# Gating products behind the result sums, a second home for their convolution, and a reordered head in the block slots of a gated MLP

## The reference

```python
x = x + conv_gated_mlp(rmsnorm(x, g_ffn), w_up, conv_w, conv_b, w_down)

def conv_gated_mlp(h, w_up, conv_w, conv_b, w_down):
    up = h @ w_up                                     # 1024 -> 2 * 2816
    pad = jnp.pad(up, ((0, 0), (1, 1), (0, 0)))
    conv = sum(pad[:, j:j + s] * conv_w[j] for j in range(3)) + conv_b
    a, b = jnp.split(conv, 2, axis=-1)
    return (jax.nn.gelu(a) * b) @ w_down
```

## Time and profile before

| | |
|---|---|
| median of 3 runs | 1733.42 us (1733.41 to 1733.48) |
| profiled execution | 1733.78 us, span 1732.0 us |
| PE busy | 1680.2 us, 97% of the span, 8873 matmuls |
| DVE busy | 1067.2 us, 62% |
| ACT busy | 833.7 us, 48% |
| POOL busy | 775.6 us, 45% |
| granted TensorE clock | full in all 40 slices |
| HBM read and written | 170.92 MB, 10.50 MB |

### The profile page before, as it was taken

One profiled execution on the slowest core, in us unless ns is written; L12 is line 12 of the kernel. 1 busy time (PEld: TensorE's weight loads), 2 busy tenths in 40 slices (PEclk: granted clock), 3 DMA queues, 4 the chain that ended last, 5 costly groups with the idle time before them and its releaser, 6 DMA issues.

```text
span 1732.0 us, 23983 instructions
## 1 busy us (share of the span) xinstructions
PE 1680.2 (97%) x8873; PEld 1444.5 (83%) x8873; DVE 1067.2 (62%) x1664; ACT 833.7 (48%) x1509; POOL 775.6 (45%) x784
## 2 busy tenths in 40 slices
PE   9999999999999899999999999999999998999998
PEld 7888888888887799988888888888888877998886
DVE  4778875533347888861146888755333587888922
ACT  4766753222344466652255766432223445666422
POOL 3443343423353677744344343343334447766422
PEclk9999999999999999999999999999999999999999
DMA  7323222224232232242352222322242332323432
GB/s 259 119 74 98 74 98 97 74 97 145 97 122 97 75 106 90 97 158 91 95 190 98 74 74 88 108 74 97 97 145 97 121 98 74 98 98 98 144 106 79
DMA packets 147317, 182.75 MB, mean 106 GB/s; under 512 B 3040, under 2 KB 130706, under 8 KB 146194
## 3 DMA queue, kind: packets, MB, share of 16 engines
q1 hardware_dynamic: 147090, 181.35, 31.5%
q10 hardware_dynamic: 128, 0.09, 0.0%
HBM read 170.92 MB, written 10.50 MB: 105 GB/s over the span
## 4 chain that ended last, share of the span: by engine, by line
PE 78%; DVE 15%; ACT 4%; issue 3%; DMA 0%; ACTq 0%; DVEq 0%; SPq 0%
PE banks L1812 15%; PE banks L1814 15%; PE banks L1813 15%; PE banks L2049 3%; PE banks L1847 3%; PE banks L1848 3%; PE banks L1849 3%; PE banks L2054 3%; PE banks L2050 3%; DVE g_f L1525 2%; DVE conv L1520 2%; DVE conv L1517 2%; PE banks L2127 2%; PE banks L2128 2%; PE banks L2129 2%
## 5 line engine op out<-in xcount | busy, mean ns | idle before, releaser
L621 POOL TENSOR_TENSOR w_lo<-raw,w_hi 128x256 fp32r<-128x256 f32 x636 | 507.5, 832 | 813.6 <-ACT w_hi L711 813.6
L1812 PE MATMUL banks<-xg_hi,w_hi 128*128 128x512 f32 x896 | 351.2, 392 | 13.3 <-issue 9.8
L1813 PE MATMUL banks<-xg_lo,w_hi 128*128 128x512 f32 x896 | 349.2, 390 | 0.0
L1814 PE MATMUL banks<-xg_hi,w_lo 128*128 128x512 f32 x896 | 348.9, 389 | 0.0
L1253 DVE TENSOR_TENSOR w_lo<-raw,w_hi 128x768 fp32r<-128x768 f32 (+2 forms) x118 | 105.7, 896 | 176.3 <-ACT w_hi L710 175.9
L1812 PEld LDWEIGHTS banks<-xg_hi,w_hi 128*128 128x128 f32 x896 | 168.3, 188 | 51.0 <-issue 12.4
L1814 PEld LDWEIGHTS banks<-xg_hi,w_lo 128*128 128x128 f32 x896 | 168.2, 188 | 35.6
L1813 PEld LDWEIGHTS banks<-xg_lo,w_hi 128*128 128x128 f32 x896 | 168.4, 188 | 33.3 <-issue 0.2
L710 ACT ACTIVATE w_hi<-raw 128x768 fp32r<-128x768 f32 (+2 forms) x119 | 87.3, 733 | 176.4 <-PE banks L1814 86.2
L711 ACT ACTIVATE w_hi<-raw 128x1280 fp32r<-128x1280 f32 (+3 forms) x119 | 158.8, 1334 | 0.0
L664 POOL TENSOR_TENSOR a_lo<-raw,a_hi 128x1024 fp32r<-128x1024 f32 (+1 forms) x56 | 109.8, 1961 | 84.9 <-ACT a_hi L1016 84.9
(11 more groups left out here) (234 smaller groups left out, 3827.7 us busy)
## 6 DMA issues: line engine op xcount, KB each, us to landing
raw<-in_w_in SPq DMA_DIRECT2D x55, 1024.0 KB, 5.1
raw<-in_w_up SPq DMA_DIRECT2D x44, 1024.0 KB, 5.1
raw<-in_w_br SPq DMA_DIRECT2D x16, 1024.0 KB, 5.0
raw<-in_w_down SPq DMA_DIRECT2D x12, 1024.0 KB, 5.0
x_spill<-x_res SPq DMA_DIRECT2D x4, 2048.0 KB, 7.4
x_res<-x_spill SPq DMA_DIRECT2D x4, 2048.0 KB, 9.3
raw<-in_w_out SPq DMA_DIRECT2D x8, 1024.0 KB, 5.0
raw<-in_w_down SPq DMA_DIRECT2D x8, 896.0 KB, 4.7
```

Of the source, the lines that this page charges most:

```text
L621: last = nc.gpsimd.tensor_tensor(w_lo[p_][:, k, :], raw[p_][:, k, :], f32(w_hi[p_][:, k, :]), ALU.subtract)
L1812: nc.tensor.matmul(out, w_hi[w][:, k, cols], x_hi[:, a, :], start=first and k == 0, stop=False)
L1813: nc.tensor.matmul(out, w_hi[w][:, k, cols], x_lo[:, a, :], start=False, stop=False)
L1814: mm = nc.tensor.matmul(out, w_lo[w][:, k, cols], x_hi[:, a, :], start=False, stop=last and k == kt - 1)
```

## The change

`x_res` is free from the spill to the reload. The convolution of b in the blocks is now computed in its second and fourth request half (`conv_of`), so that the gating product of both halves can be issued behind the two sums. In the head, ACT rounds slot 2 between the halves of slot 0, later slots as before at an iteration's end, and stages block 0 an iteration earlier; DVE subtracts the weights' low part behind the first evacuation of a slot, and does normalise, h_sum and operand_lo ahead of the convolution instead of behind it. The core of the diff:

```diff
+    def conv_of(z, half):
+        return conv[half][:, :, :] if z % 2 == 0 or z < 0 else x_res[:, 2 * half:2 * half + 2, SEQ:2 * SEQ]
...
             def reload():
                 sp.wait_ge(block_done, 7 * (l + 1) * SZ)
+                sp.wait_ge(gated_ok, (l + 1) * FSLOT * 2)
                 sp.dma_start(x_res[:, :, :], x_spill2.ap()).then_inc(reloaded2, 16)
...
             def gelu(i, half):
+                if l + i:
+                    sc.wait_ge(gated_ok, (l * FSLOT + i - 1) * 2 + (half + 1))
...
             def stage(z):
                 if z == 0:
                     sc.wait_ge(h_ok, l * KT + KT)
+                    sc.wait_ge(spilled2, 16 * l + 16)
...
             def block_hi(z, n):
+                if n == 2 and z == 0:
+                    sc.wait_ge(h_lo_pool, l * 3 + 3)
...
             def block_centre(z, half):
-                if ab == 0:
+                if ab or z == 0:
                     sc.wait_ge(gated_ok, (l * FSLOT + i - 1) * 2 + half + 1)
-                if ab:
-                    sc.wait_ge(act_ok, (l * FSLOT + i) * 2 + half + 1)
-                nc.scalar.activation(conv[half][:, :, :], half_out(z, half), ACT.Identity,
+                else:
+                    sc.wait_ge(act_ok, (l * FSLOT + i - 1) * 2 + half + 1)
+                if z == 1:
+                    sc.wait_ge(spilled2, 16 * l + 16)
+                nc.scalar.activation(conv_of(z, half), half_out(z, half), ACT.Identity,
...
             for n in range(NS):
-                if n < NS - 1:
-                    split(S_F + n + 1)
                 if n == 0:
+                    split(S_F + 1)
                     round_sum(2 * l + 1)
...
                 for half in range(2):
                     conv_centre(n, half)
                     if n % 2 == 0:
                         gelu(n // 2, half)
+                    if half == 0:
+                        if n == 0:
+                            split(S_F + 2)
+                        if n == NS - 2:
+                            stage(0)
+                        if n == NS - 1:
+                            for b in range(4):
+                                block_hi(0, b)
+                    elif n < NS - 2:
+                        if n:
+                            split(S_F + n + 2)
...
-                if ab:
-                    ve.wait_ge(conv2_ok, k)
-                    ve.wait_ge(act_ok, (l * FSLOT + i) * 2 + (half + 1))
-                    nc.vector.tensor_tensor(g_f32[:, t, :], act[half][:, :, :].rearrange("p r n -> p (r n)"),
-                                            c[:, :, :].rearrange("p r n -> p (r n)"), ALU.mult).then_inc(gated_ok, 1)
+            def multiply(z, half):
+                n = NS + z
+                k, i = conv_count(1, n // 2, half), n // 2
+                ve.wait_ge(conv2_ok, k)
+                ve.wait_ge(act_ok, (l * FSLOT + i) * 2 + (half + 1))
+                nc.vector.tensor_tensor(g_f32[:, 2 * i + half, :].rearrange("p (r n) -> p r n", r=REQS), act[half][:, :, :],
+                                        conv_of(z, half), ALU.mult).then_inc(gated_ok, 1)
...
             for z in range(1, SZ):
                 if z < SZ - 1:
                     block_adds(z + 1)
                 for half in range(2):
-                    convolve((z - 1) % 2, i, half, half_out(z - 1, half))
+                    convolve(z - 1, half, half_out(z - 1, half))
                     if z < SZ - 1 and half == 0:
                         block_low(z + 1)
                 if z == SZ - 1:
                     split(S_D)
-                    gated_lo(0)
                 block_sums(z)
-            for t in range(1, 4):
+                if z % 2 == 0:
+                    for half in range(2):
+                        multiply(z - 1, half)
+            for t in range(4):
                 gated_lo(t)
             for half in range(2):
-                convolve(1, FSLOT - 1, half, half_out(SZ - 1, half))
+                convolve(SZ - 1, half, half_out(SZ - 1, half))
                 gated_lo(4 + half)
+            for half in range(2):
+                multiply(SZ - 1, half)
             split(S_D + 1)
```

More of the change, by code:

```diff
@@ L1062, in _ @@
                         gelu(n // 2, half)
[L1063 to L1074 removed]
+                    for q in H_ACT[{(3, 0): slice(0, 3), (3, 1): slice(3, 5), (4, 0): slice(5, 7)}.get((n, half), slice(0, 0))]:
+                        operand_hi(q)
+                    if half == 0:
[9 more added lines that the diff above has]
+                            split(S_F + n + 2)
             stage(1)
@@ L1554, in block_adds @@
                     ve.wait_ge(h_lo_vector, l * 4 + 4)
-                    ve.wait_ge(h_lo_pool, l * 3 + 3)
+                    ve.wait_ge(h_t_ok, l * 4 + 4)
                 elif z < 3:
@@ L1584, in gated_lo @@
                                         f32(g_hi[:, 2 * t:2 * t + 2, :]), ALU.subtract).then_inc(g_lo_ok, 2)
+            split(S_F + 1)
+            low_sum(2 * l + 1)
+            ve.wait_ge(rms_ok, 2 * l + 2)
             for n in range(NS):
-                if n < NS - 1:
-                    split(S_F + n + 1)
-                if n == 0:
-                    low_sum(2 * l + 1)
-                    ve.wait_ge(rms_ok, 2 * l + 2)
                 for half in range(2):
                     evacuate(n, half)
-                    if n == NS - 1 and half == 0:
-                        block_adds(0)
-                    if n == NS - 1 and half == 1:
-                        block_adds(1)
-                    convolve(n % 2, n // 2, half, up_bank(n, half).rearrange("p (r n) -> p r n", r=REQS))
-                    if n == 1:
-                        for m in range(2 * half, 2 * half + 2):
-                            normalise(m)
-                    if n == 2:
-                        for m in range(4 + 2 * half, 6 + 2 * half):
+                    if 1 <= n <= 2:
+                        for m in range(4 * n + 2 * half - 4, 4 * n + 2 * half - 2):
                             normalise(m)
@@ L1609, in _ @@
                         operand_lo(H_VECTOR[2 * (n - 4) + half])
+                    if half == 0 and n < NS - 1 and n:
+                        split(S_F + n + 1)
+                    if n == NS - 2 and half == 1:
+                        block_adds(0)
                     if n == NS - 1 and half == 0:
                         block_low(0)
+                    if n == NS - 1 and half == 1:
+                        block_adds(1)
+                    convolve(n - NS, half, up_bank(n, half).rearrange("p (r n) -> p r n", r=REQS))
+                    if n % 2:
+                        multiply(n - NS, half)
             block_low(1)
```

20 lines of the change are left out of this document (3 added, 17 removed).

## The result

The changed kernel takes **1747.39 us** (1743.47 to 1747.81, 4 runs) against 1733.45 us (1733.41 to 1734.32, 4 runs) for the kernel before on the same chip: ratio 1.0074, 95% interval 1.0057 to 1.0092. It is 14 us slower. The forecast was 1730.4 us in a range of 1718 to 1740, so the time lies outside of it. The profiled execution took 1747.56 us (span 1745.8).

The account below looks back on a forecast made before the run. TensorE (PE), busy 97% of the span, was taken as the bound, so only shorter PE waits help. Terms -23.1 + 21.7 - 11.6 + 0 + 10.0 = -3.0 us from 1733.42 gave 1730.4 us, range 1718 to 1740.

Parts of the forecast that it names:

- even blocks: Blocks 2, 4, ..., 12: gating products move behind both sums, so twelve PE waits before the seventh product go; -23.1 us.
- odd blocks: Five odd blocks per layer: the late third seed makes PE wait before the fifth product; 10 x 2.17 = +21.7 us.
- head: Slots 2 to 7 of each layer: waits for weight parts shrink from 8.0 to 2.2 us per layer; -11.6 us.
- block 0: First block of each layer: 14.3 us against 14.4, so nothing; bounds -3 to +3 us for both layers.
- tail: After block 13: later reload of x_res delays the next weights; 4.4 us in layer 0, 5.6 in the last; +10.0 us.
- PE waits 2.13 us, plus 0.04 for the restart: Odd blocks, before the fifth product: PE's wait for the third seed plus restart, 2.17 us each time.
- the chain itself: Odd blocks: held fourth addition ends at 6.0 us, then ACT's rounding (1.38) and third seed (0.39), ending at 7.84.
- The hold: A DVE operation with both inputs in SBUF, issued while POOL runs, ends 0.55 us after that POOL instruction.
- rival (a): Odd blocks not held: first product beats POOL's last subtraction, started 0.15 us earlier; 21.7 us not lost, 1708.7 us; chance 0.13.
- Rival (c): Head: DVE's low part of the weights late at every slot, six slots losing 1.5 us each; 1744.6 us; chance 0.15.
- (b): Tail hidden: weights come with the first free engines, or the products run earlier; 1721 us; chance 0.10.

## Why the prediction was wrong

| term | forecast | from the profiles |
|---|---|---|
| even blocks | -23.1 | 12 x (10.13 - 12.05) = -23.0 |
| odd blocks | +21.7 | 10 x (13.74 - 10.13) = +36.1 |
| head | -11.6 | -6.4 (layer 0), -6.5 (layer 1) = -12.9 |
| block 0 | 0 | 15.65 + 15.66 - 14.43 - 14.37 = +2.5 |
| tail | +10.0 | 4.5 + 6.5 = +11.0 |
| sum | -3.0 | +13.7 (spans: +13.8) |

(The head of layer 1 is block 13 to block 0, 707.82 us against 709.77, less the 4.5 us of the tail within it.)

- **The step that failed** is the one that reads "PE waits 2.13 us, plus 0.04 for the restart", and with it "10 x 2.17 = +21.7 us". The wait was right, 2.07 us. The restart was mis-sized: it costs 1.5 us, because the granted clock falls behind a wait of this length. Shown by the extra matmuls, which leave the wait and give 14 to 15 us back, and by the longer waits of the kernel before. I had priced the restart from waits of 1.71 us, where it is 0.2 at most, and carried it to one that was 0.2 us longer than any of those. No rival spoke of the clock. With 1.5 us per odd block the sum would have been +11.6. (In the chain itself 6.05 + 1.38 + 0.39 is 7.82, not 7.84; and 2.13 is 0.05 more than 7.84 - 5.76: that is the step from the seed's end to the product, which the changed kernel has too, 7.78 and 7.83.)
- **Even blocks**, right to 0.1 us: shown by the twelve waits gone and blocks of 10.13 us.
- **The hold**, right. The fourth addition ended 5.99 us into the block, and two placements that let it start before POOL made it 0.69 us. On rival (a), which spoke of 0.15 us on POOL: the first product was held, and the additions started 0.03 us from the forecast.
- **Block 0**, forecast at nothing, cost 2.5 us. It is the same loss. PE's idle time is not more than before, but it comes in two pieces of 0.76 and 2.85 us instead of three, of which the longest was 1.99 and left the clock up. The clock of 592 to 598 us is 0.72 in the changed kernel. Two traces have the same wait with the clock up, both in layer 1: the run with 14 extra matmuls and the one with one product behind. Their block 0 lasts 14.17 us, which is near the 14.3 of the forecast; the clock costs the other 1.5 us of each 15.65.
- **Without the clock** the change would have been slightly faster. An estimate from these blocks: +13.8 - 10 x (13.74 - 12.25) - 2 x (15.66 - 14.17) = -4.1 us, against the forecast of -3.0. So one missing term made nearly all of the error.
- **Head** and **tail** were off by 1.3 and 1.0 us. The walk of the head was too careful at slots 3 to 5, where PE doesn't wait at all. Rival (c), a low part late at every slot, did not come, nor did (b): the weights landed 10.3 us after their issue, where 10.8 was taken from the row. The term of layer 1, 5.6 us, is not added up from its parts (1.2 and 3.1) in the prediction; it measured 6.5.
- The clock also fell once in each tail: the granted clock is 0.59 from 772.8 to 777 us and 0.62 from 1640 to 1644.5, behind waits of 1.93 and 2.7 us. In layer 0 that adds nothing to be seen: with the products behind the additions the clock stayed up behind a wait of 1.92 us there, and block 13 to block 0 took 707.71 us, against 707.82. In layer 1 no run separates it, so that a part of the 6.5 us may be the clock's.
- By the 436 GB/s of the Trainium skill (DMA: Bandwidth & Descriptors, section Where 436 GB/s comes from) the tail would have cost about 3 us; it cost 11. The same section says that for transfers from HBM a limit of about 358 GB/s binds, which the prediction left out; as an estimate from it, 3.0 MB need 8.4 us. The trace is near the lower rate: from 762 to 770.9 us, up to the landing of the weights, the DMA queues moved 370 GB/s.
- The range was too narrow by 7 us. It held bounds for block 0, head and tail, but none for the largest positive term, whose chain was read from rows while its last link, the engine's pace behind the wait, was taken as fixed.

What stays open: why a wait of this length costs the clock in most blocks and not in all. Waits of 1.93 us in two odd blocks of layer 1 left it up in one run, 1.99 us did in block 0 of the kernel before, 2.85 us in two blocks 0, and 1.8 us cost it in 11 of 12 even blocks of another. In the head, on the other hand, all nine waits of 1.76 to 1.81 us in the kernel before and its variants left it up. The length of the wait alone does not decide it. No run separated what else does.

## What to carry to other kernels

A stall that moves from one place to another is not priced by its length alone. One unharmed stall of the same length proves little: the trace of before had one of 1.99 us with the clock up, and the new ones of 1.92 us all lost it. What could be relied on was the length that passed every time in the same kind of place (twelve of 1.71 us in front of a product). Beyond such a length, put one clock loss per stall into the range, 1.5 us here, and look at the granted clock and the pace of the matmuls behind the stall. Before an operation is moved on one engine, list which of its neighbours have both inputs in SBUF and where POOL's instructions start; the same work put a few instructions later (behind the additions instead of in front of them) was worth 35 us here. And in a queue that works in order, put what another engine needs soonest (the seed) ahead of what waits longest (the rounding): that alone gave 29 us.

## What the runs showed of the hardware

- The granted clock can fall behind a short stall. Twelve waits of 1.71 us in the kernel before left it at 1.00 and cost 0.2 us beyond themselves, and ten of 1.4 us left it up too. Waits of 1.8 to 2.0 us cost the clock in 32 of 36 even blocks, those of 1.92 and 1.93 us in 18 of 20 odd ones, and those of 2.85 us in 12 of 14 blocks 0. The loss was 1.5 us at 1.8, 1.9 and 2.0 us and did not grow with the wait. In block 0 it varied: 1.2 to 1.5 us in ten, and 2.6 to 2.7 in two, whose clock stayed down for longer (16.81 and 16.89 us instead of 14.17). The Trainium skill (TensorE: Matmul & The Clock Gate, section What's actually happening) says that the chip gates this clock to half by how busy the engine has been; the trace agrees: matmul starts 0.21 us apart instead of 0.12, and a granted clock of 0.57 to 0.66 in stretches of both levels.
- Idle time can be filled to advantage. Four matmuls whose result nothing uses took 0.5 us of the wait and saved 13.9 and 15.5 us in two different kernels.
- The hold turns on 0.3 us. A DVE operation with two SBUF inputs takes 0.69 us if issued before POOL's instruction, and ends 0.54 to 0.55 us behind it if issued 0.3 us after its start (2.63 and 2.90 us). The Trainium skill (SBUF — State Buffer, section Who interferes with whom) says that such an operation contends with a GpSimd instruction that reads SBUF; the trace agrees, and the rows add what the order is worth: 0.69 against 2.63 us for the same addition.
